# Moving the gather of item 2 ahead of the item loop, and the first clamp ahead of one weight split, in a hybrid DeltaNet and mixture-of-experts block

## The reference

```
h = x + mixer(rms_norm(x))          # gated DeltaNet + short convolution, merged by gates
h = h + moe(rms_norm(h))            # 4 of 32 experts for each token
out = rms_norm(h)

# moe, for the 128-row block xb of expert e:
gu   = xb @ w_gate_up[e] + b_gate_up[e]                  # 1024 -> 2048
gate = min(gu[:, :1024], 7);  up = clip(gu[:, 1024:], -7, 7)
hid  = (up + 1) * gate * sigmoid(1.702 * gate)
y    = hid @ w_down[e] + b_down[e]                       # 1024 -> 1024
out[token] += weight[token, e] * y                       # softmax over the 4 chosen logits
```

## Time and profile before

| | |
|---|---|
| median of 3 runs | 1866.62 us (1864.3 to 1869.83) |
| profiled execution, its own time | 1861.92 us |
| its span, first to last instruction | 1860.2 us |
| mean granted PE clock | 0.993 |
| PE busy | 97% |
| DVE, ACT, POOL busy | 79%, 59%, 21% |

### The profile page before, as it was taken

One profiled execution on the slowest core, in us unless ns is written; L12 is line 12 of the kernel. 1 busy time (PEld: TensorE's weight loads), 2 busy tenths in 40 slices (PEclk: granted clock), 3 DMA queues, 4 the chain that ended last, 5 costly groups with the idle time before them and its releaser, 6 DMA issues.

```text
span 1860.2 us, 23887 instructions
## 1 busy us (share of the span) xinstructions
PE 1807.2 (97%) x8636; PEld 1504.8 (81%) x8636; DVE 1471.4 (79%) x1101; ACT 1104.0 (59%) x906; POOL 390.3 (21%) x329
## 2 busy tenths in 40 slices
PE   7999999899999998999999999999999999999995
PEld 6888888798888886888888888888888888888883
DVE  4236666765344688899999999999999999999996
ACT  4223563333332446777777777777777777777771
POOL 0000112410000016321322321322222232232230
PEclk9999999999999998999999999999999999999998
DMA  4323423005572638899999999999999999999975
GB/s 162 112 91 109 163 89 116 18 7 181 205 236 91 237 140 313 321 379 383 358 373 383 354 371 381 368 363 378 378 347 379 382 349 375 380 355 372 384 292 242
DMA packets 129630, 507.80 MB, mean 273 GB/s; under 512 B 26183, under 2 KB 26391, under 8 KB 95476
## 3 DMA queue, kind: packets, MB, share of 16 engines
q1 hardware_dynamic: 118276, 490.69, 69.1%
q0 software_dynamic: 9136, 16.27, 2.3%
q10 hardware_dynamic: 2176, 0.26, 0.1%
HBM read 491.93 MB, written 32.02 MB: 282 GB/s over the span
## 4 chain that ended last, share of the span: by engine, by line
PE 87%; DVE 6%; DMA 2%; ACT 2%; issue 2%; POOL 1%; SPq 0%; POOLq 0%; ACTq 0%; DVEq 0%
PE PB L2328 12%; PE PB L2327 12%; PE PB L2330 12%; PE PB L2246 11%; PE PB L2351 6%; PE PB L2348 6%; PE PB L2349 6%; PE PB L1931 4%; PE PB L1933 4%; PE PB L1932 4%; PE PB L2064 2%; PE PB L2317 2%; PE PB L2305 1%; PE PB L2311 1%; PE PB L2211 1%
## 5 line engine op out<-in xcount | busy, mean ns | idle before, releaser
L516 DVE TENSOR_TENSOR mlo<-mraw,mhi 128x2048 fp32r<-128x2048 f32 x384 | 908.2, 2399 | 54.4 <-ACT mhi L512 52.7
L512 ACT ACTIVATE mhi<-mraw 128x2048 fp32r<-128x2048 f32 x384 | 721.8, 1914 | 111.8 <-PE PB L2330 111.0
L2327 PE MATMUL PB<-mhi,xgT_hi 128*128 128x512 f32 x1024 | 402.9, 393 | 0.7 <-DVE mlo L516 0.7
L2328 PE MATMUL PB<-mlo,xgT_hi 128*128 128x512 f32 x1024 | 400.2, 391 | 0.0
L2330 PE MATMUL PB<-mhi,xgT_lo 128*128 128x512 f32 x1024 | 274.4, 390 | 0.0
L2327 PEld LDWEIGHTS PB<-mhi,xgT_hi 128*128 128x128 f32 x1024 | 192.8, 188 | 41.1 <-issue 0.8
L2330 PEld LDWEIGHTS PB<-mhi,xgT_lo 128*128 128x128 f32 x1024 | 192.6, 188 | 40.6
L2328 PEld LDWEIGHTS PB<-mlo,xgT_hi 128*128 128x128 f32 x1024 | 192.9, 188 | 39.6
L2348 PE MATMUL PB<-mhi,hT_hi 128*128 128x512 f32 x512 | 202.6, 396 | 1.1 <-DVE hT_lo L1829 1.1
L2349 PE MATMUL PB<-mlo,hT_hi 128*128 128x512 f32 x512 | 199.9, 390 | 0.0
L888 POOL TENSOR_TENSOR glu<-glu 128x1024 f32<-128x1024 f32 x32 | 76.7, 2396 | 529.6 <-DVE glu L1824 529.6
(11 more groups left out here) (359 smaller groups left out, 2551.1 us busy)
## 6 DMA issues: line engine op xcount, KB each, us to landing
mraw<-in_w_gate_up_dram SPq DMA_DIRECT2D x256, 1024.0 KB, 8.3
mraw<-in_w_down_dram SPq DMA_DIRECT2D x128, 1024.0 KB, 8.0
raw<-in_w_in_dram SPq DMA_DIRECT2D x28, 1024.0 KB, 5.1
qkvT<-in_w_in_dram SPq DMA_DIRECT2D x8, 1024.0 KB, 5.1
expert_rows_scratch<-zeros SPq DMA_DIRECT2D x4, 2048.0 KB, 11.5
mraw<-expert_rows_scratch SPq DMA_DIRECT2D x6, 1024.0 KB, 11.6
qkvT<-in_w_o_gdn_dram SPq DMA_DIRECT2D x4, 1024.0 KB, 6.4
qkvT<-in_w_o_sconv_dram SPq DMA_DIRECT2D x4, 1024.0 KB, 5.1
```

The lines of the kernel that those rows point to most:

```text
L512: nc.scalar.activation(mhi[split_slot(m)][:], mraw[:, raw_slot(m), :], ACT.Copy).then_inc(e_h, 1)
L516: nc.vector.tensor_tensor(mlo[split_slot(m)][:], mraw[:, raw_slot(m), :], mhi[split_slot(m)][:].bitcast(F32), ALU.subtract).then_inc(e_l, 1)
L2327: pe.matmul(gate_up_bank[:, n, :], xgT_hi[:, k, :], w_hi[:, n, :], start=False, stop=False)
L2328: pe.matmul(gate_up_bank[:, n, :], xgT_hi[:, k, :], w_lo[:, n, :], start=False, stop=False)
```

## The change

It has three parts. On POOL, the gather of item 2 is issued ahead of item 0's `hidden`, and the gather inside the loop moves from the top of iteration i to its end, for item i + 3 in place of i + 2. There is so one gather more in all, of item `last` + 2. On ACT, the hi part of item 1's tokens and the sigmoid of item 0 stand ahead of the two mixing copies. On DVE, the clamps, the lo part of the tokens and the product of item 0 stand ahead of the split of chunk 9 (m = 13) and of the mixing subtraction.

```
# POOL
                         nc.gpsimd.tensor_tensor(mix_w[:], mix_w[:], by_choice[:, :, k, :], ALU.add).then_inc(s_mixw, 1)
+                    pool.wait_ge(s_tx, 1)
+                    gather(2)
                     hidden(0)
...
                     with pool.Fori(0, last) as i:
-                        pool.wait_ge(s_tx, i + 1)
-                        gather(i + 2)
                         pool.wait_ge(s_th, i + 1)
                         hidden(i + 1)
                         scatter(i)
+                        pool.wait_ge(s_tx, i + 2)
+                        gather(i + 3)
                     pool.sem_inc(s_stored, 1)
-                    pool.wait_ge(s_xg, 16 * last + 16)
+                    pool.wait_ge(s_xg, 16 * last + 32)
# ACT
                     for m in range(10, 14):
                         weights_hi(act, -1, m)
+                    tokens_hi(1)
+                    sigmoid(0)
                     act.wait_ge(s_mixw, TOPK)
                     for n in range(2):
                         nc.scalar.activation(mix3[:, :, n * E:(n + 1) * E], mix_w[:], ACT.Copy).then_inc(s_mix3, 1)
-                    tokens_hi(1)
-                    sigmoid(0)
# DVE
-                    for m in range(11, 14):
+                    for m in range(11, 13):
                         weights_lo(dve, -1, m)
                     dve.wait_ge(s_store, 16 * TT)
                     clamp(0, first=True)
+                    tokens_lo(1)
+                    gated(0)
+                    weights_lo(dve, -1, 13)
                     dve.wait_ge(s_mix3, 2)
                     nc.vector.tensor_tensor(mix3[:, :, 2 * E:], ...)
-                    tokens_lo(1)
-                    gated(0)
```

## The result

The changed kernel takes 1857.12 us (median of 6 runs, 1854.49 to 1857.49) against 1865.49 for the one before (6 runs, 1863.35 to 1869.83). The ratio is 0.995, with a 95% interval of 0.9936 to 0.9963. That is 8.4 us, 0.45%, clear of the noise. The forecast was -2.9 us, 1863.7, with a range down to 1858.0. Its profiled execution took 1855.72 us, with a span of 1854.0, against 1861.92 and 1860.2.

A forecast was written before the change was run, and what follows sets the result against it. PE was taken as the bound, busy 97% of the span, with two waits at the loop's start and DVE waiting for reads at the end. -5.3 - 1.7 + 4.1 = -2.9 us gives 1863.7 us, range 1858.0 to 1869.0.

The forecast's parts named there:

- Hole B: Start of the loop: PE waits 3.53 us, till 737.13, for the rows of item 2; with its low clock 5.32 us.
- Gain B: 5.3 us, 5.2 to 5.4: Start of the loop: the earlier gather of item 2 on POOL removes PE's wait for its rows and the low clock behind.
- The end: Behind the last scatter: the extra gather on POOL delays SP's reads; loss 4.1 us, 2.6 to 4.2.
- by this rule the end costs the 4.1: Behind the last scatter: DVE and GpSimd lock a shared port pair for a full instruction, the loser blocked; loss 4.1 us.
- The prediction's own sign of being wrong: Behind the last scatter: the forecast is wrong if SP's reads start less than 2 us later.
- Hole A: Start of the loop: PE waits 3.54 us for item 0's second clamp; falls to about 1.9, gain 1.7 us, 1.5 to 1.9.
- the low clock is not in this: Start of the loop: PE's wait, now 1.9 us, is followed by full clock, as an idle of 2.87 us was.
- The alternative in the same paragraph: Start of the loop: should the clock fall at 702.4, chunk 8 hides both stands and PE reaches chunk 16 at 728.99.
- The loop: Inside the loop: POOL's work keeps its order, turned by one place, and PE is full; zero change.
- The first: Rival: the end is free, the extra gather slips in or sooner release was worth nothing; -7.0 us, 1859.6; chance 0.13.
- the clock's fall: Rival at chunks 9 and 10: PE's stands make the clock fall, costing at most 2.98 us; sum +0.3, 1866.9; chance 0.08.
- the 10.2 of the prediction: Rival at the end: s_stored held till the extra gather has landed; end costs 10.2 us, sum +3.2, 1869.8; chance 0.05.

The follow-up runs named there:

- engine release: Changed kernel with s_stored raised by a small memset on POOL behind the extra gather; SP's first DMA came 4.1 us later than in the kernel before.
- held release: Changed kernel with s_stored raised only when the extra gather has landed; median 1861.29 us against 1855.12 for the changed kernel on that chip.
- the order alone: Kernel before with only the ACT and DVE part of the change, POOL as before; 1868.02 us (12 runs), ratio 1.0007.
- the gather alone: Kernel before with only the POOL part of the change; 1856.71 us (7 runs), ratio 0.9946.
- with the release: Kernel before with only the POOL part, and SP's reads released once the last scatter has landed, ahead of the extra gather; 1856.55 us, ratio 0.9942.

## Why the prediction was wrong

**Hole B, mis-sized.** The step "Gain B: 5.3 us, 5.2 to 5.4" failed in its size. The mechanism was right: the gather went early, the wait is gone, chunk 17 was ready. In the profile I had it was worth 17.17 - 11.79 = 5.4. But in the two other profiles of before the same stretch holds 8.0 and 8.7 us. The profiled execution was a quick one of its kind, 4.7 us under the median of three runs, and I carried that difference over to the changed kernel as an offset. It was not all offset: the two other profiles took 2.3 us more, and their stretch of hole B alone holds 2.6 and 3.3 us more, in the term that the change removes. With 8.0 for hole B and 1.5 for the end, the same sum gives -8.2 us. A wait that ends with a chain on POOL among DVE's splits had no fixed length here (3.53, 4.94, 6.41 us), and the 5.2 to 5.4 from rows of one execution did not bound it.

**The end, mis-sized.** "Loss: 4.1 us" measured 1.3 us at SP's first DMA and 1.5 at the last instruction, below the lower bound of 2.6. The step that failed is that `s_stored` waits until the gather's DMA instruction has run on the engine. The lengths of copy, step and DMA instruction were forecast well. The engine release shows that all the rest of the step was right: it costs 4.1. So an operation of POOL did wait for DVE's split, and still "by this rule the end costs the 4.1" did not follow from it. The prediction's own sign of being wrong, reads that start less than 2 us later, came true.

**Hole A, right in size, and worth little by itself.** Forecast 1.7; PE's first bias matmul came 1.7 us sooner counted from t0, and the stretch to chunk 16 is 2.0 us shorter. The clamps ended at 702.0, the split of chunk 9 went first, `hidden(0)` behind it, chunk 10 at 711. Wrong was "the low clock is not in this": it fell behind 1.84 us of wait. The alternative in the same paragraph covered that, PE at chunk 16 at 728.99 against the measured 728.45. What I missed is the dependence: alone, the order gains nothing, since hole B grows (10.45 us of wait).

**The loop, right.** 1062.38 against 1062.43 us: turning the loop's order by one place cost nothing.

**Rivals.** The first, a free end, came nearest, and still gave 1859.6; the end was not free, but its 1.3 to 1.5 us lie at that rival's border of 1.4. In the changed order the clock's fall cost nothing that the splits would not have cost (29.14 us with it, 29.12 without). The held release costs 5.2 us where it is made true, not the 10.2 of the prediction.

## What to carry to other kernels

A stall that ends with a chain on GpSimd amid VectorE's two-input work should be priced from several executions; where the timed runs spread and the profiled one lies outside them, look for the spread in the very term that the change removes. An extra instruction ahead of a release costs what the releasing queue has to wait for, not what the engine has to do: ask whether the increment hangs on an engine's instruction or on the sequencer. And time won at one wait is lost at the next when another chain ends that one: the order alone gained nothing, while the gather alone gained all that could be told.

## What the runs showed of the hardware beyond that

A semaphore increment of POOL's own sequencer took effect 1.6 us ahead of the start of a DMA instruction that stands before it in the program (1810.14 against 1811.76), and 0.7 us behind the copy that POOL's program waits for; hung on a memset, the release reached SP 0.14 us behind the memset's start.

TensorE's clock fell to half (1.2 of 2.4 GHz) behind waits of 3.54 and of 1.84 us. In the first case it fell while PE still waited (the granted clock is 0.72 from 703 to 704 us, and PE starts at 704.13), in the second when PE was at work again, 0.5 to 1.1 us after its start in the seven profiles that have this wait (an estimate from the granted clock in stretches of 1 us). It did not fall behind 1.31 us, nor behind 2.87 in the earlier trace rows, where the granted clock stays at 1.00. Behind the same wait of 3.5 us the low clock cost between 1.4 us (25.04 us from the bias to chunk 16 in the gather alone) and 3.0 (26.56 with the release). So the length of that one wait did not settle by itself whether the clock fell, nor for how long.
